# A two-layer diffusion step on one core: the input projection in three rounded products, its first loads moved forward, and one activation table for Ln and Exp

## The reference

```python
def mixer_inputs(h, w_in, conv_w, a_log, dt_bias, q_gain, k_gain):
    p = jnp.einsum('bld,de->ble', h, w_in)
    qa, ka, va, qkvd, z, a, bt = jnp.split(p, SPLIT_POINTS, axis=-1)
    ...
    qkvd = jax.nn.silu(centred_conv(qkvd, conv_w))     # five taps over the tokens
    qd, kd, vd = jnp.split(qkvd, (DN_QK, 2 * DN_QK), axis=-1)
    qd = l2_normalize(qd.reshape(B, L, DN_HEADS, DK)) * (DK ** -0.5)
    kd = l2_normalize(kd.reshape(B, L, DN_HEADS, DK))
```

## Time and profile before

| what | value |
|---|---|
| three executions | 2160.69, 2165.2, 2166.62 us |
| the profiled execution | 2164.64 us |
| its span, first to last instruction | 2162.9 us |
| mean granted TensorE clock | 0.926 |
| busy: TensorE, VectorE, ScalarE, GpSimd | 1829.2, 1251.1, 968.5, 213.2 us |
| moved by DMA | 376.39 MB |

### The profile page before, as it was taken

One profiled execution on the slowest core, in us unless ns is written; L12 is line 12 of the kernel. 1 busy time (PEld: TensorE's weight loads), 2 busy tenths in 40 slices (PEclk: granted clock), 3 DMA queues, 4 the chain that ended last, 5 costly groups with the idle time before them and its releaser, 6 DMA issues. The chain is left out here.

```text
span 2162.9 us, 36690 instructions
## 1 busy us (share of the span) xinstructions
PE 1829.2 (85%) x13621; PEld 1328.0 (61%) x13622; DVE 1251.1 (58%) x1843; ACT 968.5 (45%) x1449; POOL 213.2 (10%) x267
## 2 busy tenths in 40 slices
PE   6599988999699299999955999899996939999991
PEld 0255547888544088888842654488884528888881
DVE  0318425766433389696654284266663448999664
ACT  0221273343323088686632214633432328888651
POOL 0000002322100100000020000132220010000002
PEclk8699998999799599999987999999997969999996
DMA  9621107000276599798734220000004049999844
GB/s 394 247 78 40 42 2 263 3 2 2 72 269 239 223 364 398 285 393 335 291 124 129 78 80 0 12 12 3 2 2 139 30 165 361 400 401 403 327 175 175
DMA packets 96320, 376.39 MB, mean 174 GB/s; under 512 B 14478, under 2 KB 35030, under 8 KB 65478
## 3 DMA queue, kind: packets, MB, share of 16 engines
q1 hardware_dynamic: 80486, 316.76, 39.3%
q0 software_dynamic: 8496, 30.94, 3.8%
q10 hardware_dynamic: 7216, 26.97, 3.1%
HBM read 332.86 MB, written 41.78 MB: 173 GB/s over the span
## 5 line engine op out<-in xcount | busy, mean ns | idle before, releaser
L1809 DVE TENSOR_TENSOR expert_w_lo<-shared,expert_w_hi 128x2048 fp32r<-128x2048 f32 x192 | 430.5, 2286 | 47.4 <-ACT expert_w_hi L1751 46.7
L1751 ACT ACTIVATE expert_w_hi<-shared 128x2048 fp32r<-128x2048 f32 x192 | 359.9, 1910 | 59.9 <-PEq L141 56.7
L1693 PE MATMUL ps<-expert_w_hi,expert_x_hi 128*128 128x512 f32 x592 | 232.6, 393 | 5.1 <-DVE expert_x_lo L1805 5.1
L1695 PE MATMUL ps<-expert_w_hi,expert_x_lo 128*128 128x512 f32 x592 | 232.3, 392 | 0.0
L1694 PE MATMUL ps<-expert_w_lo,expert_x_hi 128*128 128x512 f32 x592 | 232.2, 392 | 0.0
L495 PE MATMUL ps<-shared,projection_hT 128*128 128x512 f32 (+1 forms) x480 | 181.6, 536 | 0.7 <-ACT kT L448 0.7
L518 PE MATMUL ps<-projection_hT,shared 128*128 128x512 f32 x384 | 169.0, 593 | 0.0
L495 PEld LDWEIGHTS ps<-shared,projection_hT 128*128 128x128 f32 x480 | 92.4, 194 | 82.9 <-issue 75.4
L1693 PEld LDWEIGHTS ps<-expert_w_hi,expert_x_hi 128*128 128x128 f32 x592 | 112.4, 190 | 29.4 <-issue 5.9
L1695 PEld LDWEIGHTS ps<-expert_w_hi,expert_x_lo 128*128 128x128 f32 x592 | 112.3, 190 | 23.5
L1694 PEld LDWEIGHTS ps<-expert_w_lo,expert_x_hi 128*128 128x128 f32 x592 | 112.3, 190 | 23.4
(11 more groups left out here) (330 smaller groups left out, 3177.8 us busy)
## 6 DMA issues: line engine op xcount, KB each, us to landing
shared<-in_w_gate SPq DMA_DIRECT2D x64, 1024.0 KB, 7.3
shared<-in_w_up SPq DMA_DIRECT2D x64, 1024.0 KB, 8.6
shared<-in_w_down SPq DMA_DIRECT2D x64, 1024.0 KB, 9.0
setup_m_ada_ring<-in_w_ada SPq DMA_DIRECT2D x24, 1024.0 KB, 10.5
shared<-in_w_in SPq DMA_DIRECT2D x10, 2048.0 KB, 8.0
y_table<-expert_y ACTq DMA_DIRECT2D x37, 512.0 KB, 8.8
y_table<-zero SPq DMA_DIRECT2D x1, 12800.0 KB, 41.1
qkv<-in_w_ada SPq DMA_DIRECT2D x11, 1024.0 KB, 4.9
```

The lines of the kernel that those rows point to most:

```text
L1693: pe.matmul(bank, hi, w_hi[:, j, w], start=first, stop=False)
L1695: return pe.matmul(bank, lo, w_hi[:, j, w], start=False, stop=last)
L1751: act.activation(w_hi[:, j, :], raw[:, j, :], ACT.Copy).then_inc(w_hi_done, 1)
L1809: dve.tensor_tensor(w_lo[:, j, :], raw[:, j, :], w_hi[:, j, :].bitcast(F32), ALU.subtract).then_inc(w_lo_done, 1)
```

## The change

- **Products.** h is split as it leaves PSUM: ScalarE copies both halves of a tile to a high part (fp32r), VectorE subtracts for the low part. The weights are split in blocks of 128 or 136 columns for 8 k-slices at once (128 x 1024 or 1088 elements): high part on ScalarE (in the first layer's four QG blocks on VectorE), low part on VectorE, written over the raw block. There are 22 such blocks a layer: 4 QG, 2 KVG, 12 channel tiles, 4 ZG. Each product is three fp32r matmuls. For a channel tile the columns are no longer 512 and 128, but 256 (context and the first latent tile) and 384.
- **Convolution.** The first tap is on ScalarE (Copy with a scale per partition); VectorE keeps four. ScalarE copies the raw channels in three pieces. The turns are interleaved behind channel tiles 7, 8 and 9.
- **Head.** The QG weights are loaded at the end of the setup phase (layer 0) or in the combine phase (layer 1), there with the shift and scale rows too; layer 1's sums of squares are made by ScalarE in the combine phase. KVG is loaded only once all five tiles of h are made, as it lands where shift and scale lie.
- **Tables.** An explicit load of the set that has Ln and Exp both, after each Silu (setup, projection, tail) and at the start of combine; the Ln ahead of need in the tail goes.

```diff
+def load_ln_exp(act):
+    act.add_instruction(mybir.InstLoadActFuncSet(name=act.bass.get_next_instruction_name(), act_func_set_id=LN_EXP_SET))
...
+def load_first(eng, A, G, l, queries, rows):
+    if queries:
+        src = A.w_in[l:l + 1].rearrange("a (k p) n -> p (a k) n", p=P)
+        eng.dma_start(G.first_view, src[:, :, Q0:Q0 + 512]).then_inc(G.q_in, 16)
+    if rows:
+        for n, dst in enumerate(G.mod_view):
+            eng.dma_start(dst, A.mod_rows[l][:, n * D:(n + 1) * D].partition_broadcast(P)).then_inc(G.mod_in, 16)
...
     def dve_take(self, dve, t):
-        dve.wait_ge(self.turned, 2 * t + 2)
-        dve.tensor_copy(self.hT[:, 4:8, t * P:(t + 1) * P],
-                        self.G.ps[:, 2 * (t % 2) + 1, :].rearrange("p (k n) -> p k n", k=4)).then_inc(self.dve_took, 1)
+        for half in range(2):
+            dve.wait_ge(self.act_took, 2 * t + half + 1)
+            dve.tensor_tensor(self.lo_of(t, half), self.turned_half(t, half), self.hi_of(t, half).bitcast(F32),
+                              ALU.subtract).then_inc(self.dve_took, 1)
...
+        def low_block(dve, n):
+            dve.wait_ge(s_["w_hi"], n + 1)
+            dve.tensor_tensor(raw_block(n, ring_r), raw_block(n), high_block(n).bitcast(F32), ALU.subtract).then_inc(s_["w_lo"], 1)
...
+                    if g == KVG:
+                        sp.wait_ge(ada.h_ready, NT)
...
                 for ct in range(CT):
                     g = C0G + ct // 4
+                    pe.wait_ge(s_["w_lo"], CB0 + ct + 1)
                     if ct >= 2:
                         pe.wait_ge(s_["chan_taken"], 2 * (ct - 1))
-                    w = lambda k: ring[:, g % RS, k, (ct % 4) * P:(ct % 4 + 1) * P]
-                    for k in range(KD):
-                        pe.matmul(G.ps[:, 2 * (ct % 2), :], w(k), hT[:, k, P:T], start=(k == 0), stop=(k == KD - 1))
-                    for k in range(KD):
-                        mm = pe.matmul(G.ps[:, 2 * (ct % 2) + 1, 0:P], w(k), hT[:, k, 0:P], start=(k == 0), stop=(k == KD - 1))
+                    w_hi, w_lo = high_block(CB0 + ct), raw_block(CB0 + ct, ring_r)
+                    outs = [(G.ps[:, 2 * (ct % 2) + b, 0:(until - t) * P], t, until) for b, t, until in ((0, 0, 2), (1, 2, NT))]
+                    for k in range(KD):
+                        for out, t, until in outs:
+                            pe.matmul(out, w_hi[:, k, :], h_hi[:, k, t * P:until * P], start=(k == 0), stop=False)
...
                     mm.then_inc(s_["chan"], 1)
+                    for n in turns_after.get(ct, ()):
+                        q_turn(n)
...
+                def high(n):
+                    g = blocks[n][0]
+                    act.wait_ge(*((G.q_in, 16 * (l + 1)) if g == QG else (loaded[g % RS], landed[g])))
+                    if CB0 + 2 <= n < ZB0:
+                        act.wait_ge(s_["chan"], n - CB0 - 1)
+                    elif n >= ZB0:
+                        act.wait_ge(s_["chan"], CT - 4 + (n - ZB0) + 1)
+                    act.activation(high_block(n), raw_block(n), ACT.Copy).then_inc(s_["w_hi"], 1)
...
+                    act.activation(cvs[:, ct % RC, :], raw[:, ct % RC, 0:OUTL], ACT.Copy, scale=cwT[:, ct:ct + 1]).then_inc(s_["tap0"], 1)
+                    if ct + 2 < CT:
+                        high(CB0 + ct + 2)
...
+                if l in SETUP_LAYERS:
+                    dve.wait_ge(G.q_in, 16 * (l + 1))
+                    for n in range(QB):
+                        dve.tensor_copy(high_block(n), raw_block(n)).then_inc(s_["w_hi"], 1)
+                    for n in range(QB):
+                        low_block(dve, n)
                 for t in range(NT):
                     ada.dve_tile(dve, t)
+                    if t == 0 and l not in SETUP_LAYERS:
+                        for n in range(QB):
+                            low_block(dve, n)
...
                 for ct in range(CT):
+                    for n in lows_at[ct]:
+                        low_block(dve, n)
...
                     conv(ct)
                     if 1 <= ct <= NT:
                         head_rows(ct - 1)
```

More of the change, by code:

```diff
@@ L319, with __init__ @@
 class Adaln:
[L322 to L325, removed]
+    def __init__(self, ph, G, A, l, which, hi_of, lo_of, rows, junk):
+        self.ph, self.G, self.A, self.l, self.which, self.hi_of, self.lo_of = ph, G, A, l, which, hi_of, lo_of
+        self.shift, self.scale = G.mod_view
         self.rows, self.nrow, self.junk = rows, rows.shape[1], junk
[L327 to L330, removed]
+        self.rstd = G.rstd[:, l, :]
+        self.rs = ph.sem("rstd_ready")
@@ L339, in act_stats @@
     def act_stats(self, act):
[L340 to L348, removed]
@@ L490, in rows @@
                         if t == 0:
-                            pe.wait_ge(loaded[g % RS], landed[g])
+                            pe.wait_ge(s_["w_lo"], {QG: QB, KVG: CB0, ZG: len(blocks)}[g])
                         if r >= 4:
                             pe.wait_ge(s_["row_taken"], r - 3)
+                        out, n = G.ps[:, 4 + r % 4, 0:width[g]], width[g]
                         for k in range(KD):
-                            mm = pe.matmul(G.ps[:, 4 + r % 4, 0:width[g]], hT[:, k, t * P:(t + 1) * P],
-                                           ring[:, g % RS, k, 0:width[g]], start=(k == 0), stop=(k == KD - 1))
@@ L522, in _ @@
-                pe.wait_ge(s_["cw_ready"], 1)
-                pe.wait_ge(s_["prepped"], NT)
-                pe.wait_ge(s_["ctx_in"], 16)
-                for n in range(NTURN):
+                            hi, lo = h_hi[:, k, t * P:(t + 1) * P], h_low(k, t, t + 1)[:, 0, :]
+                            w_hi, w_lo = high_of(g)[:, k, 0:n], ring_r[:, g % RS, k, 0:n]
+                            pe.matmul(out, hi, w_hi, start=(k == 0), stop=False)
+                            pe.matmul(out, hi, w_lo, start=False, stop=False)
@@ L526, in _, with q_turn @@
+                            mm = pe.matmul(out, lo, w_hi, start=False, stop=(k == KD - 1))
+                        mm.then_inc(s_["rowp"], 1)
+                def q_turn(n):
+                    if n == 0:
+                        pe.wait_ge(s_["prepped"], NT)
+                        pe.wait_ge(s_["ctx_in"], 16)
                     if n >= 4:
@@ L604, in _ @@
                         ada.act_take(act, t + 1)
+                    if t == NT - 1:
+                        for n in range(QB, QB + KVB):
+                            high(n)
                     take_row(t)
@@ L726, in _ @@
                         head_rows(ct - 1)
-                for n in range(1, NTURN, 2):
-                    take_turn(dve.tensor_copy, dve, n, "turn_v")
                 dve.wait_ge(s_["row_taken"], 2 * NT)
@@ L1932, in build @@
         G.carve = carve
+        G.first_view = carve(0, (KD, 512))
+        G.mod_view = [carve(KD * 512 + n * 2 * D, (2, D)) for n in range(2)]
+        G.rstd = sb("rstd", [P, layers, NT])
+        G.q_in, G.mod_in = (top.enter_context(nc.semaphore(n)) for n in ("first_weights_in", "first_rows_in"))
         G.y_zero = top.enter_context(nc.semaphore("y_zero"))
```

192 lines of the change are left out of this document (134 added, 58 removed).

## The result

The changed kernel took 2101.1, 2105.66, 2103.25 and 2105.23 us, a median of 2104.24 against 2164.11 for four of the kernel before: ratio 0.9717, with a 95% interval of 0.9704 to 0.9730. Predicted were 2100 and a range of 2078 to 2130. The profiled execution took 2101.1 us, the shortest of the four; its span, first to last instruction, is 2099.4. So the two profiled spans differ by 63.5 us where the medians differ by 59.9.

The account below looks back on a forecast made before the run. TensorE was taken to bound the QG rows, KVG rows and conv channels, with ScalarE's table loads making TensorE wait in Z. Layer 0 -31 and layer 1 -34 gave 2164.6 - 65 = 2100 us, range 2078 to 2130.

Parts of the forecast that it names:

- Prices of products: Projection: three fp32r matmuls priced by width, channel tile 7.0 us for 8.66; QG and KVG rows 9.9 us less.
- theory A: Forecast for the 128 and 512 column split: fp32r matmul costs width plus some 0.01 us, 0.069 for 128 columns.
- Conv loop: Conv channels: VectorE's low parts behind head rows delay TensorE at tiles 5 to 8; 95 us for 103.9, 9 less.
- Turns: Handovers after the conv channels go into the loop; 4.2 us of idle TensorE for 7.6, 3.4 less.
- Z: Z stage: without table loads TensorE becomes the bound at 7.9 us a tile; 40.5 us for 51.2, 10.8 less.
- Tables elsewhere: Tail: its table loads lie under the output projection's matmuls, so sparing them was put at nothing.
- Combine: Combine and layer 1's head: 2 us for 4 MB beside gathers, plus 3 and 12: 17.0 for 17.7, 0.7 less.
- Layer 0's head: Before layer 0's first QG row: weights land about 79, VectorE splits four blocks in 8.8 us; 2 us more.
- 1: Rival: VectorE paces the whole conv loop, each channel tile near 9.9 us, or idle gaps halve the clock; 2130 to 2148; chance 0.12.
- 2: Rival: table loads stay where they were, Z stays with ScalarE; 2122 us; chance 0.08.
- 3: Rival: fp32r products of 256, 272 and 384 columns cost as much as 512; 2204 us; chance 0.05.
- 4: Rival: VectorE's conv chain overlaps better, combine hides its 4 MB, head at its lower bound; 2080 us; chance 0.1.

Follow-up runs that it names:

- experiment 4: Changed kernel with a channel tile's columns as 128 and 512: 2120.49 us; as 64 and 512, last 64 context tokens left out: 2118.34 us.
- experiment 7: Changed kernel, head rows in 13 pieces over channel tiles 0 to 8: turns after tiles 9 and 10, 2113.88 us; after 10 and 11, 2092.12 us.
- experiment 6: Changed kernel with all eleven turns after channel tile 11, as before the change: 2105.3 us (0.9728).
- experiment 1: Kernel before, with explicit table loads after each Silu and at combine's start, and the tail's early Ln removed: 2155.01 us (0.9955).
- experiment 2: Changed kernel without the explicit loads of the common table, everything else kept: 2129.67 us (0.9835).
- experiment 5: Changed kernel, loads for layer 1's head issued in combine only once the second tile's gathers have landed and been scaled: 2105.06 us (0.9726).
- experiment 9: Changed kernel with tile 0's low part and first QG row moved ahead, five gather buffers, prefetch behind the first scaled tile: 2098.85 us (0.9691).

## Why the prediction was right, and where it was off

- **Prices of products: right.** QG and KVG rows -9.6 and -9.9 for -9.9; a channel tile 7.1 for 7.0. The step that took the price below 512 columns by width held because the change never goes below 256, which was not known: at 128 it is 0.115 us instead of theory A's 0.069 (experiment 4). No run shows the fixed 0.012 us that my prices below 512 columns add to the width (0.114 + 0.012 for 272); the runs showed 0.126 us for 272 columns, 0.295 for 256 and 384 together and 0.23 for 512. The 128 columns in fp32 gave no warning: one of their records took 1.79/16 = 0.112 us, close to the 0.115, but also close to a quarter of the 0.429 for 512. In layer 0 the KVG load landed 5.4 us after its issue at 104.93, yet the rows had little to spare: ScalarE splits those blocks only behind its copy of the fourth QG row, at 119.9, VectorE is done at 123.5, and TensorE takes them at 124.7.
- **Conv loop: right, and by the mechanism given.** 94.8 us for 95; VectorE's period 9.76 for 9.9; the low parts of tiles 6, 7 and 8 came 45.1, 54.8 and 64.6 us after the first channel matmul, for 45.3, 55.2 and 65.1. TensorE is held up at tiles 6 to 8 and not after (predicted 5 to 8), at 8 by the turns and the head rows, not by the low part. Experiment 7 confirms it: with the head rows spread the waits go. Missing was the clock, which took another 1.7 us at tile 6. It did no harm to the sum, since VectorE's low parts set the pace there and the next wait took it up.
- **Turns: right in sum** (4.2 us idle for 7.6), though experiment 6 shows that the transposes also cost the loop some microseconds, so that the move is worth 1.2 to 2.7 and not 3.4.
- **Z: mis-sized.** 41.8 for 40.5 (my terms add up to 40.7). The step was 2.5 us for the norms' matmuls with their waits, beside 5.44: rows are taken 8.2 us apart, not 7.9, of which 0.1 is the row's own matmuls (5.6). Start-up was near: 8.1 us to the first copy for 8.4. Condition and bound were right (experiments 1 and 2): TensorE 40.07 of 41.78.
- **Tables elsewhere: off.** "The tail's table loads lie under the output projection's matmuls" is not quite so: they were worth 2.3 us in experiment 1 and 3 in experiment 2.
- **Combine: the step that failed.** I took 2 us between nothing and 11.4, since "only tiles 1 to 4 slip". It was 4.85, and the first tile slips too: its gathers landed 2.2 us later than before. The delay is handed on: with three buffers the fourth tile's gathers can be issued only when the first tile is added, and they then meet the rest of the prefetch and land 4.9 us late. Experiment 5 shows the meeting: with the first three tiles in time again, the fourth was scaled 25.8 us after combine's start, 21.7 before the change. Five buffers with the prefetch behind the first scaled tile give 29.1 (experiment 9). The rest of that head was right: 2.9 us for 3, 11.2 for 12.
- **Layer 0's head:** +1.05 for +2. The weights landed at 80.1 (79 expected), the four copies and subtractions took 7.0 us, not 8.8: a copy is 0.6 us, below my bounds of 0.9 to 1.2.
- **Rivals.** 1 is refuted as a whole (tiles 6 to 8 took 8.2 to 10.9 us, the others 7.1 to 7.8), though its halved clock did occur at one tile and at Z. 2 is refuted by 48 loads. 3 is refuted at these widths alone. 4's "combine hides its 4 MB" is false here and true in experiment 9.
- **The sum: close in part by luck.** The spans differ by 63.5 us for 65. Z gave 2.8 us less than forecast in the two layers and combine 2.9. Against them stand 1.8 us better in the two heads, 0.5 in the conv stages, and 2.3 in "all else", which I had at nothing and of which 1.3 are the clock in layer 1's mixer. By the medians (59.9 us) the forecast missed by 4 to 5 us.

The 1.8 us less in layer 1's mixer show in all kernels with the changed projection but those of experiments 2 and 6. That of experiment 6 has the slow first matmuls again (2.85 us to the next group); in that of experiment 2 the transposes behind Z lose as much as is gained. What stays open is why the clock is lower at the mixer's start in some kernels and not in others, and the other 0.5 us.

## What to carry to other kernels

When an engine's work grows by a piece that another engine waits for (here the low parts), ask first what stands ahead of it in the same list: cutting 5 us blocks into pieces and moving the turns to a place of waiting gave 12 us at no less work. Two changes that each relieve one of two nearly equal bounds must be costed together. A prefetch beside gathers cost 5 to 6 us here while later gathers waited for a buffer, whether it was issued ahead of them or behind the second tile: the delay of one gather is handed on to those behind it. With a buffer for each tile and the prefetch behind the first, x was ready earlier than before the change.

## What the runs showed of the hardware that I had not expected

- An fp32r matmul with its own 128x128 weights took at least 0.115 us (64 and 128 columns), 0.126 for 272 and 0.23 for 512, so that 640 columns as 256 and 384 cost 7.1 us a tile, as 128 and 512 8.2.
- A wait of 2.07 us was followed, 1 us after its end, by 3.3 us at a granted clock of 0.50, one of 4.2 at once by about 5: the matmuls in them took 1.7 and 2.4 us longer. The first QG row had a clock of 0.93 with transposes ahead of it and 0.59 with a wait of 1.4 us there. The clock also reached stages that no edit touched: 1.3 us at the mixer's start (0.73 and 1.00), 1.8 us in the transposes behind Z (0.61 and 1.00).
- GpSimd's tensor-tensor of 128x160 took mostly 1.07 us or more beside VectorE's taps and 0.47 after them; the taps took 1.093 us in that kernel's channels, 0.888 in the changed kernel.
